# The first four levels of a triangular inverse as products of 32 by 32 instead of 64 by 64

## The reference, cut to what matters

```python
k_beta = k * beta[..., None]
a_strict = jnp.where(idx[:, None] > idx[None, :],
                     jnp.einsum('bhncd,bhnsd->bhncs', k_beta, k) * decay, 0.0)
tri = a_strict + jnp.eye(c, dtype=jnp.float32)
u = lax.linalg.triangular_solve(tri, v * beta[..., None], left_side=True, lower=True, unit_diagonal=True)
w = lax.linalg.triangular_solve(tri, k_beta * jnp.exp(gc)[..., None], left_side=True, lower=True,
                                unit_diagonal=True)
```

## Time and profile before

| | |
|---|---|
| timed runs, median | 2683.03 us (2679.43 to 2683.88) |
| the profiled execution's own time | 2683.2 us |
| its span, first to last instruction | 2681.4 us |
| PE busy | 2448.3 us, 91% of the span |
| DVE busy | 1728.4 us, 64% |
| ACT busy | 1121.2 us, 42% |
| the inverse, from its first matmul to its last update | 185.56 to 232.38 us |
| DVE in it (185.5 to 232.5) | 28.39 us busy |
| PE in it | 40.15 us busy |

### The profile page before, as it was taken

The page is one execution under the profiler, slowest core; times in us unless marked ns, Lnnn a source line. Parts: engine busy times, 40 slices in busy tenths (PEclk is TensorE's granted clock), DMA queues, the critical chain, the costliest instruction groups (busy, mean ns, idle before and its releaser), DMA issues. The chain is left out here.

```text
span 2681.4 us, 47280 instructions
## 1 busy us (share of the span) xinstructions
PE 2448.3 (91%) x19417; PEld 2350.2 (88%) x19417; DVE 1728.4 (64%) x2539; ACT 1121.2 (42%) x1600; POOL 130.1 (5%) x159
## 2 busy tenths in 40 slices
PE   6878589997986899979998999999999989999998
PEld 6777589997865799979998889899999988898998
DVE  4765267775473577757775565677777755756776
ACT  4543243334362433334334655433433346554332
POOL 2321000000000000000003000000000030000000
PEclk9988789998897799989999999999999999999999
DMA  7320145554801355526446233545455462234542
GB/s 200 121 80 17 35 157 188 188 187 122 176 27 51 122 178 186 188 80 204 160 154 167 98 103 111 172 162 170 143 188 182 132 178 95 95 122 161 185 161 78
DMA packets 294983, 370.23 MB, mean 138 GB/s; under 512 B 15321, under 2 KB 263634, under 8 KB 294802
## 3 DMA queue, kind: packets, MB, share of 16 engines
q1 hardware_dynamic: 289584, 354.85, 40.6%
q0 software_dynamic: 4880, 13.13, 2.7%
q10 hardware_dynamic: 370, 0.11, 0.0%
HBM read 360.20 MB, written 7.86 MB: 137 GB/s over the span
## 5 line engine op out<-in xcount | busy, mean ns | idle before, releaser
L302 PE MATMUL psum_banks<-source_high,weights_high 128*128 128x272 f32 (+1 forms) x3680 | 1083.1, 294 | 71.0 <-DVE weights_low L1540 23.2
L303 PE MATMUL psum_banks<-source_low,weights_high 128*128 128x272 f32 (+1 forms) x3680 | 1067.6, 290 | 0.0
L304 PE MATMUL psum_banks<-source_high,weights_low 128*128 128x272 f32 (+1 forms) x3680 | 1067.4, 290 | 0.0
L302 PEld LDWEIGHTS psum_banks<-source_high,weights_high 128*128 128x128 f32 x3680 | 713.3, 194 | 82.4 <-DVE weights_low L1540 25.3
L303 PEld LDWEIGHTS psum_banks<-source_low,weights_high 128*128 128x128 f32 x3680 | 713.7, 194 | 0.7
L304 PEld LDWEIGHTS psum_banks<-source_high,weights_low 128*128 128x128 f32 x3680 | 712.6, 194 | 0.0
L1540 DVE TENSOR_TENSOR weights_low<-weight_ring,weights_high 128x2048 fp32r<-128x2048 f32 x102 | 235.7, 2313 | 178.4 <-ACT weights_high L1533 177.7
L302 PE MATMUL psum_banks<-hidden_high,weights_high 128*128 128x272 f32 (+1 forms) x1216 | 349.7, 288 | 0.0
L304 PE MATMUL psum_banks<-hidden_high,weights_low 128*128 128x272 f32 (+1 forms) x1216 | 348.4, 287 | 0.0
L303 PE MATMUL psum_banks<-hidden_low,weights_high 128*128 128x272 f32 (+1 forms) x1216 | 347.2, 286 | 0.0
L1013 DVE TENSOR_TENSOR weights_low<-weight_ring,weights_high 128x2048 fp32r<-128x2048 f32 x131 | 292.9, 2287 | 74.1 <-ACT weights_high L1007 74.0
(11 more groups left out here) (416 smaller groups left out, 2872.2 us busy)
## 6 DMA issues: line engine op xcount, KB each, us to landing
weight_ring<-ffn_w_in SPq DMA_DIRECT2D x88, 1024.0 KB, 6.4
weight_ring<-w_in SPq DMA_DIRECT2D x48, 1024.0 KB, 5.2
weight_ring<-ffn_w_out SPq DMA_DIRECT2D x44, 1024.0 KB, 4.9
weight_ring<-moe_w_gate SPq DMA_DIRECT2D x32, 1024.0 KB, 6.0
weight_ring<-moe_w_up SPq DMA_DIRECT2D x32, 1024.0 KB, 6.9
weight_ring<-moe_w_down SPq DMA_DIRECT2D x32, 1024.0 KB, 5.0
weight_ring<-gdn_w_in SPq DMA_DIRECT2D x16, 1024.0 KB, 6.0
weight_ring<-w_branch SPq DMA_DIRECT2D x12, 1024.0 KB, 5.0
```

What stands on the lines that cost most here:

```text
L302: pe.matmul(out, w_hi, x_hi, start=start, stop=False)
L303: pe.matmul(out, w_hi, x_lo, start=False, stop=False)
L304: return pe.matmul(out, w_lo, x_hi, start=False, stop=stop)
```

## The change

The corners become a function of the level: tiles of 32 in levels 0 to 3, where the blocks that arise are of 4, 8, 16 and 32, and tiles of 64 in level 4 as before. The products and the updates use it alike. Level 5, the copies of ACT, the masks of GpSimd and all semaphores stay.

```diff
-        corner = [slice(0, P // 2), slice(P // 2, P)]
+        corners = lambda lev: [slice(at, at + max(32, 4 << lev)) for at in range(0, P, max(32, 4 << lev))]
...
                 def per_block(b, lhs, rhs):
                     for h in range(H):
-                        for s in corner:
+                        for s in corners(lev):
                             ins = pe.matmul(bank2(b)[s, h, s], lhs(h)[s, s], rhs(h)[s, s], start=True, stop=True)
                     return ins
...
                         inv[t].begin(dve, 4 * lev + 3)
                         if lev < LEVELS - 1:
                             b = 2 << lev
-                            for s in corner:
+                            for s in corners(lev):
                                 x = left(X[:, t], s, b)
                                 dve.tensor_tensor(x, x, left(bank2(4 * t + 2), s, b), sub)
```

## The result

The changed kernel takes 2695.48 us (median of 5 runs, 2694.37 to 2697.05), where the kernel before took 2680.18 us (median of 5, 2678.48 to 2683.88): a ratio of 1.0057 [1.0044, 1.007]. It is 15.3 us slower, and outside the range of the prediction. (The prediction started from three runs of the kernel before with a median of 2683.03; started from 2680.18, its forecast would be 2678 and its range would end at 2690.) The profiled executions stand 12.3 us apart (2695.48 and 2683.2), and the inverse accounts for all of it, 13.5 us: it lasts from 185.28 to 245.55 us, 60.3 us, where it lasted 46.8 (185.56 to 232.38).

What follows compares the result with a forecast made beforehand. PE's chain was taken to bound the kernel. Cheaper products against dearer updates gained 1.2 us in level 0, 0.8 in level 1, lost some in level 2, gained 0.9 in level 3: 2683.0 - 2.05 = 2681 us, range 2676 to 2693.

Steps and rivals of the forecast that it cites:

- The loop: Level 1 of the inverse: three products and two updates in line, 5.7 us where it was 6.5, gain 0.8.
- rival 1: Products of levels 0 to 3: matmuls paid one by one, 64 in 1.87 us, about +18 us, 2701; chance 0.09.
- The product of 0.50 us: Products of levels 0 to 3: four corners at once, 16 rounds of 31 ns, 0.50 us instead of 0.93.
- Rival 2: PE's clock in the inverse doesn't hold with the work halved: 2683, 2687 or 2693 us by how long; chance 0.16.
- The updates: DVE's updates in levels 0 to 3: eight instructions each, 1.95 us with a hand-over where it was 1.52, +0.43.

Runs made afterwards that it cites:

- the run with the first products: Kernel before, with only the first product of either chunk in levels 0 to 3 split into matmuls of 32 rows and 64 columns: 2681.31 us, ratio 1.0004.
- instructions only: Kernel before, updates included, with each 64 by 64 tile of levels 0 to 3 as two matmuls of 32 rows and 64 columns: 2692.73 us.
- two tiles of four: Changed kernel with only every second tile of 32 multiplied in levels 0 to 3, half of the diagonal blocks left out: 2683.00 us.
- 64 columns: Changed kernel with 64 columns of data instead of 32 in each matmul of levels 0 to 3, same instructions: 2695.80 us.

## Why the prediction was wrong

**The step that failed.** It is the pace of the products in the sum: "The loop becomes 0.05 + 0.50 + 1.00 + 0.21 + 1.95 + 1.95 + 0.03 = 5.7 us". It lets three products, and all six in a level, run at 0.50 us each, 768 instructions in 5.7 us. At 3.46 us for 256 the supply needs 3 x 3.46 = 10.4 us for them, and level 1 took 10.65. The instructions were counted, in rival 1, and dismissed by an average: "the queue that brings it is in use for 0.3% of the engines' time". That number is true and is still 0.3% after. It is a mean over 16 DMA engines and the whole span, while the fetch is one packet at a time, with a wait before and after it. What mattered was its time from one block to the next, and "its quickest delivery is not shown" was the sentence to which a range should have been tied.

**The product of 0.50 us: nearly right, where it is supplied.** In the full clock 60 MATMULs take 0.72 us with the last one's 0.19, 9.0 ns from start to start, 0.57 for 64, so four tiles do run at once:

```profile
190.84 0.72 PE L1753 MATMUL psum_banks<-a_strict,inverse_pair 32*32 32x32 f32 x60
...
187.57 1.08 PE L1753 MATMUL psum_banks<-a_strict,inverse_pair 32*32 32x32 f32 x64
188.42 0.93 PE L1753 MATMUL psum_banks<-inverse_pair,a_strict 32*32 32x32 f32 x51
```

At the lower clock a product takes 0.85 us (187.57 to 188.42), as predicted.

**Rival 1: near by its sum, wrong by its mechanism.** It gave 2701 us for matmuls paid one by one at 29 ns. They are not: 9 ns. The rule of the Trainium skill that the prediction weighed ("TensorE: Matmul & The Clock Gate", no start-to-start under about 25 ns) gave a loss of about 13 us, and 15.3 came. That is no support for it: its floor is for the time from one matmul to the next, and a run of 60 undercuts it by a factor of nearly three. Only the mean over a starved block, 3.47 us for 128 matmuls, is 27 ns. The run with the first products shows the difference: 128 instructions close together cost nothing where the block has slack.

**Rival 2, the clock: it came, and cost about 1 us.** I expected it to hold; it fell at 192.82. In the starved blocks it costs nothing: they take 3.46 us at the full clock (instructions only) and 3.47 at half. Where it shows is level 4, which lasted until 239.06 (238.64 + 0.42) from 231.60, 7.46 us where it had 6.5; levels 4 and 5 together are 0.94 us longer. Whether it fell for PE's stops or for the smaller tiles is open: it stayed low without a stop in the run with two tiles of four, and rose and fell in the runs with stops and 64 columns. For level 1 at the low clock the prediction had 6.85 us; that run, with half of the tiles, has 6.88.

**The updates: right.** 1.95 predicted, 1.99 measured (202.38 to 204.37, in the rows of the timeline), and 3.3 us in the stage when they come alone (the last 1.3 of it in level 3, where the clock was low for a part in both).

**The sum of the loss.** 60.27 - 46.82 = 13.45 us in the stage: 12.5 in levels 0 to 3, where the supply sets the pace, 0.9 in levels 4 and 5 by the clock. The updates' 3.3 us are hardly on top: with updates of before (instructions only) levels 0 to 3 take 45.7 us, with the new ones 46.3, and DVE works during the stops. The medians (2692.73 against 2695.48 and 2695.80) leave room for up to 3 us.

## What to carry to other kernels

Count the instructions of a stage, not only their work: where 256 instructions of TensorE (128 matmuls and their weight loads, as the trace counts them) would run in less than about 3.5 us, the stream that brings them set the pace here, and splitting matmuls finer only added to it. In a trace it looks like idle time on "issue" in the middle of a product, at a fixed number of instructions. A mean use of a queue says nothing on a resource that serves one request at a time; ask for its time from one request to the next.

## What the runs showed of the hardware that I had not expected

- The kernel before stood at the edge: four of its products are 256 instructions in 4 x 0.93 = 3.73 us, 0.27 us above the shortest block. A cut into twice as many instructions leaves a block at most some 1.9 us of work.
- Four tiles of 32 by 32 run at 9 ns a matmul in full clock and 13.6 at half (60 in 1.03 us, less 0.23 for the last).
- The fetch can be held up. In the block from 213.08 to 218.19, 5.11 us instead of 3.47, DMA was moving 195 GB/s (a weight panel of 1 MB). The longest stops of the runs with 64 columns and with instructions only (3.67 and 2.92 us) lie beside the same panel. That the panel is the cause was not tried.
- PE working on two tiles of 32 rows only, 5.54 of 6.88 us busy, was granted one half of its clock in that whole level.
